# Small products of constants at the borders of stages, in a norm and between an attention's first scores, on one Trainium2 core

## What is computed

```python
def first_block(x, c, ctx, ...):
    h  = modulate(rms_norm(x, g_attn), sh_a, sc_a)
    rq, rk, rv, rg, qn, qp, kn, kp, mv = head_group_inputs(h, w_in, ...)
    y_ret = retention_mix(rq, rk, rv, rg, ...)
    y_mla = blocked_attention(q_m, concat([k_mc, k_m]), concat([mvc, mv]))
    x_mid = x + gt_a * (concat([y_ret, y_mla]) @ w_out)
    x = x_mid + gt_f * sq_relu_mlp(modulate(rms_norm(x_mid, g_ffn), sh_f, sc_f), w_ff1, w_ff2)
    return rms_norm(x, g_final)

def second_block(x, meta_tokens, ...):          # two layers
    h = rms_norm(h_res, norm_gain[li])
    f_in, q, k, v, gate = split(h @ w_in[li])
    f_out = fourier_mixer(f_in, w_fourier[li])
    s = q @ k.T * scale; p = softmax(s)          # two components for each head
    o = (p[0] - lam * p[1]) @ v
    y = concat([f_out, rms_norm(o)]) * silu(gate)
    h_res = h_res + y @ w_out[li]
```

## Time and profile before

| | us |
|---|---|
| median of 3 runs | 2792.8 (2792.77 to 2797.52) |
| the profiled execution | 2796.85 |
| its span, first to last instruction | 2795.1 |
| mean granted clock of TensorE | 0.972 |

### The profile page before, as it was taken

The page is one execution under the profiler, slowest core; times in us unless marked ns, Lnnn a source line. Parts: engine busy times, 40 slices in busy tenths (PEclk is TensorE's granted clock), DMA queues, the critical chain, the costliest instruction groups (busy, mean ns, idle before and its releaser), DMA issues. The chain is left out here.

```text
span 2795.1 us, 35915 instructions
## 1 busy us (share of the span) xinstructions
PE 2642.2 (95%) x14429; PEld 2265.9 (81%) x14429; DVE 1434.5 (51%) x2019; ACT 1054.1 (38%) x1846; POOL 456.4 (16%) x283
## 2 busy tenths in 40 slices
PE   5999869899889999999999999989999999989999
PEld 1877766899777888888888999779989999768987
DVE  5743682333457666666658423347743522326751
ACT  3412443444245334333344222157722222227740
POOL 0002201332000000000000000048820000008940
PEclk8999979999989999999999999999999999999999
DMA  5531101000211112112111233232122113233222
GB/s 234 181 132 48 41 5 53 16 1 1 106 39 53 38 61 61 44 48 61 46 53 48 92 82 82 78 78 47 43 101 106 48 42 84 57 106 74 55 83 84
DMA packets 67570, 189.46 MB, mean 68 GB/s; under 512 B 8016, under 2 KB 26832, under 8 KB 66512
## 3 DMA queue, kind: packets, MB, share of 16 engines
q1 hardware_dynamic: 67408, 187.22, 21.9%
HBM read 146.79 MB, written 16.97 MB: 59 GB/s over the span
## 5 line engine op out<-in xcount | busy, mean ns | idle before, releaser
L2649 DVE SCALAR_TENSOR_TENSOR res<-ps,gates,res 128x1024 f32<-128x1024 f32 x120 | 148.6, 1279 | 100.0 <-PE ps L2773 100.0
L1285 PE MATMUL ps<-h_hi,pf_wh 128*128 128x346 f32 (+2 forms) x800 | 187.8, 338 | 0.3
L1285 PE MATMUL ps<-h_lo,pf_wh 128*128 128x346 f32 (+2 forms) x800 | 183.0, 333 | 0.0
L2508 ACT ACTIVATE wo_wh<-ff_raw 128x512 fp32r<-128x512 f32 x120 | 75.3, 628 | 280.3 <-DVE ff_raw L2619 114.2
L1921 DVE TENSOR_REDUCE da_negmax<-ps 128x1 f32<-128x1040 f32 x136 | 167.9, 1236 | 20.9 <-PE ps L1775 14.1
L1906 POOL TENSOR_TENSOR da_E<-da_E,da_F 128x1040 f32<-128x1040 f32 x68 | 164.6, 2421 | 5.7
L2773 PE MATMUL ps<-ff_h_hi,wo_wh 128*128 128x512 f32 x512 | 157.8, 389 | 1.4 <-DVE res L2649 1.3
L1818 PE MATMUL ps<-da_aT,v 128*128 128x128 f32 (+1 forms) x1224 | 158.1, 275 | 0.7 <-ACT qk L1878 0.7
L2773 PE MATMUL ps<-ff_h_lo,wo_wh 128*128 128x512 f32 x512 | 157.7, 389 | 0.0
L2773 PE MATMUL ps<-ff_h_hi,wo_wl 128*128 128x512 f32 x512 | 157.6, 389 | 0.0
L1292 PE MATMUL ps<-h_hi,pf_wl 128*128 128x346 f32 (+2 forms) x800 | 152.4, 338 | 0.0
(11 more groups left out here) (540 smaller groups left out, 6154.9 us busy)
## 6 DMA issues: line engine op xcount, KB each, us to landing
ff_raw<-w_ff SPq DMA_DIRECT2D x48, 512.0 KB, 3.5
ada_w<-w_ada SPq DMA_DIRECT2D x16, 1024.0 KB, 7.3
ff_raw<-w_in SPq DMA_DIRECT2D x20, 512.0 KB, 4.1
pf_raw<-w_in SPq DMA_DIRECT2D x20, 512.0 KB, 4.2
wo_raw<-w_out SPq DMA_DIRECT2D x18, 512.0 KB, 4.4
residual_spill<-res SPq DMA_DIRECT2D x16, 520.0 KB, 3.1
st_q<-st_q_rounded SPq DMA_DIRECT2D x32, 260.0 KB, 5.1
ada_w<-w_ada SPq DMA_DIRECT2D x4, 2048.0 KB, 16.8
```

The lines of the kernel that those rows point to most:

```text
L1285: pe.matmul(bank(i * 2 + s, s)[c], wh[:, s, q * P:(q + 1) * P], x(q)[:, a:a + ln], start=(q == 0 and n == 0), stop=False)
L2508: act.activation(ring(wh, i), src, ACT.Copy).then_inc(s_hi, 1)
L2649: last = dve.scalar_tensor_tensor(out=res[:, m, :], in0=k.ps[:, b:b + 2, :].rearrange("p c w -> p (c w)"), scalar=gate[:, m:m + 1], in1=re ...
```

## The change

A new function issues `n` products of `k.ones` by `k.ident` into a bank. It is called at the start of stages (`before`), at their end (`behind`, in `gemm` after a wait for the last evacuation of slot 0, in `gemm_tokens` after a wait for the first five), in the norm's sums, in the feed-forward at both ends, at the start of the latent attention, and in the differential attention behind the second component's scores of the first three groups and behind the last product. In the norm the increment of `s_ssq` stays on the same product but moves into the loop.

```diff
+def busy(pe, k, bank, n):
+    for _ in range(n):
+        pe.matmul(k.ps[:, bank, 0:P], k.ones[:], k.ident[:], start=True, stop=True)
 def gemm(..., split_token=False):
+         ..., before=0, behind=0, idle_bank=7):
+                busy(pe, k, idle_bank, before)
                 loop(pe, body)
+                if behind:
+                    pe.wait_ge(freed[0], NI)
+                    busy(pe, k, 0, behind)
                 if follow:
                     follow.sums(pe, 0)
 def gemm_tokens(..., also=None):
+         ..., before=4, behind=0):
+                busy(pe, k, 7, before)
                 for g, ts in enumerate(groups):
...
+                if behind:
+                    pe.wait_ge(out_lo if split else out_hi, 5)
+                    busy(pe, k, 4, behind)
 # diff_attention, TensorE's loop
                         if i < NG:
                             pv(i, 0)
+                        else:
+                            busy(pe, k, 1, 4)
                         continue
...
                     if g < NG:
                         scores(g, 1)
+                    if i < 0:
+                        busy(pe, k, 7, 6)
 # latent_heads
+                busy(pe, k, 7, 22)
                 for g in range(NG + LAG):
 # KeptNorm.sums
             for t in range(self.NT):
                 mm = pe.matmul(k.ps[:, 5, 2 * t:2 * t + 2], src[:, t * P:(t + 1) * P], k.ones[:, 0:2], ...)
-        mm.then_inc(self.s_ssq, 1)
+            if i == 1:
+                mm.then_inc(self.s_ssq, 1)
+            busy(pe, k, 2, (2, 4)[i])
 # feed_forward
+                busy(pe, k, 5, 13)
                 first()
...
+                pe.wait_ge(join.s_x, 6)
+                busy(pe, k, 0, 5)
```

More of the change, by code:

```diff
@@ L1062, in gemm @@
 def gemm(nc, k, name, w_rows, MT, KT, xh, xl, chunks, evac_act=None, evac_dve=None, preloaded=False, then=None, load=None, norm=None,
-         follow=None, store_tile=None, side=None, first_raw=None, ahead=None, split_first=None, split_next=None, chunks_at=None, late=None, stored=None, split_token=False):
+         follow=None, store_tile=None, side=None, first_raw=None, ahead=None, split_first=None, split_next=None, chunks_at=None, late=None, stored=None, split_token=False, before=0, behind=0, idle_bank=7):
     NI = max(MT // 2, 1)
@@ L1321, in token_tiles, with gemm_tokens @@
     return k.sb(f"{name}_wh", [P, 3, N], k.ring0 + 12 * N, F32R), k.sb(f"{name}_wl", [P, 3, N], k.ring0 + 16384, F32R)
-def gemm_tokens(nc, k, name, w_rows, KT, N, xh, xl, toks, out, preloaded=False, then=None, side=None, row_scale=None, also=None):
+def gemm_tokens(nc, k, name, w_rows, KT, N, xh, xl, toks, out, preloaded=False, then=None, side=None, row_scale=None, also=None, before=4, behind=0):
     groups = [list(range(g, min(g + 5, len(toks)))) for g in range(0, len(toks), 5)]
@@ L2288, in latent_attention @@
     at0 = h0 + 4 * 5152 + MH * LT * 4
-    gemm(nc, k, "uk", rows(d["w_uk"]), MH, 2, lambda q: kh[:, q, :], lambda q: kl[:, q, :], call, preloaded=True, norm=norm, then=("mv", lambda q: d["w_mv"][q % 2 * P:(q % 2 + 1) * P, :], MH * MV, 3), side=keys,
+    gemm(nc, k, "uk", rows(d["w_uk"]), MH, 2, lambda q: kh[:, q, :], lambda q: kl[:, q, :], call, preloaded=True, norm=norm, before=14, behind=4, then=("mv", lambda q: d["w_mv"][q % 2 * P:(q % 2 + 1) * P, :], MH * MV, 3), side=keys,
          evac_act=copy_out(lambda m, a, w: kraw[:, m, a:a + w] if isinstance(m, int) else kraw[:, bass.ds(m, 1), a:a + w], call))
@@ L2292, in latent_attention @@
                 lambda q, a: kh[:, q, a:a + P], lambda q, a: kl[:, q, a:a + P],
-                list(range(0, LT, P)), lambda t: (v[:, t, :],), preloaded=True, then=("uq", rows(d["w_uq"]), 3 * P, 2))
+                list(range(0, LT, P)), lambda t: (v[:, t, :],), preloaded=True, behind=4, then=("uq", rows(d["w_uq"]), 3 * P, 2))
     qpe = k.sb("q_pe", [P, MH, L], k.res0 - 512)
@@ L3627, in project @@
             silu(act, m - 12, s, i, banks, freed, first)
-    gemm(nc, k, f"pf{li}", rows(d["w_in2"], R0), 20, KD, XH, XL, cx, evac_act=project, evac_dve=times_root, preloaded=True, norm=norm, late=norm,
+    gemm(nc, k, f"pf{li}", rows(d["w_in2"], R0), 20, KD, XH, XL, cx, evac_act=project, evac_dve=times_root, preloaded=True, norm=norm, late=norm, before=7, behind=6,
          split_first=k.split[f"pf{li}"], chunks_at=lambda m: cg if isinstance(m, int) and m >= 12 else cx,
@@ L3637, in second_layer @@
                 lambda q, a: hh[:, q * L2 + a:q * L2 + a + P], lambda q, a: hl[:, q * L2 + a:q * L2 + a + P],
-                list(range(0, L2, P)), lambda t: (v[:, t, :],), preloaded=True, side=stacks, row_scale=norm.rc, also=last_silu)
+                list(range(0, L2, P)), lambda t: (v[:, t, :],), preloaded=True, side=stacks, row_scale=norm.rc, also=last_silu, before=2, behind=8)
     yb = qk
@@ L3660, in second_layer @@
         own = [k.sb(f"pf1_first_{part}", [P, KD * P], p0 + 4096 * x, F32R)[:] for x, part in enumerate(("hi", "lo"))]
-        more = dict(follow=follow, then=("pf1", rows(d["w_in2"], 20 * P), KD * P, 2), split_next={1: own}, stored=follow.s_kept,
+        more = dict(follow=follow, behind=5, then=("pf1", rows(d["w_in2"], 20 * P), KD * P, 2), split_next={1: own}, stored=follow.s_kept,
                     store_tile=lambda m: (spill[:, m:m + 1, :], k.res[:, m:m + 1, :]) if isinstance(m, int)
@@ L3712, in project @@
         last.then_inc(freed, 1)
-    gemm(nc, k, "ina", rows(d["w_ina"]), 8, KD, XH, XL, cx, norm=n1, preloaded=True, split_first=tuple(per_slot(t) for t in k.split["ina"]), then=("inb", rows(d["w_inb"]), KD * P, 2),
+    gemm(nc, k, "ina", rows(d["w_ina"]), 8, KD, XH, XL, cx, norm=n1, before=12, behind=4, preloaded=True, split_first=tuple(per_slot(t) for t in k.split["ina"]), then=("inb", rows(d["w_inb"]), KD * P, 2),
          evac_act=project,
@@ L3717, in first_block @@
                   a0, a0 + 8 * L, k.rot1, 6)
-    gemm(nc, k, "inb", rows(d["w_inb"]), 6, KD, XH, XL, call, preloaded=True, side=BesideKeys(AdaRest(k, d, ada, k.res0, "ada2", 10, {0: [0, 1], 1: [2], 2: [3], 3: [4], 4: [5]}), turns),
+    gemm(nc, k, "inb", rows(d["w_inb"]), 6, KD, XH, XL, call, preloaded=True, before=4, behind=4, idle_bank=6, side=BesideKeys(AdaRest(k, d, ada, k.res0, "ada2", 10, {0: [0, 1], 1: [2], 2: [3], 3: [4], 4: [5]}), turns),
          then=("rv", rows(d["w_rv"]), RH * RDV, 3),
@@ L3743, in first_block @@
                                 gain=lambda q: k.a1[:, 2, q:q + 1], shift=lambda q: k.mod[:, 24 + q, 0:1])], y0, F0 + 72 * L)
-    mix_out(nc, k, d["xT"], "wo1", rows(d["w_out"]), yh, yl, cx, k.gates[:, 0, :], L, norm=split, first_raw=k.raw["wo1"], preloaded=True, follow=n2, then=("ff", rows(d["w_ff"]), KD * P, 2), split_next={})
+    mix_out(nc, k, d["xT"], "wo1", rows(d["w_out"]), yh, yl, cx, k.gates[:, 0, :], L, norm=split, first_raw=k.raw["wo1"], preloaded=True, follow=n2, before=12, then=("ff", rows(d["w_ff"]), KD * P, 2), split_next={})
     n2.keep_tiles(k.sb("ffn_in_kept", [P, 4, 4, L // 2], F0 + 40 * L), fh, fl)
```

2 lines of the change are left out of this document (1 added, 1 removed).

## The result

| | before | after |
|---|---|---|
| median, us | 2793.6 (2792.77 to 2797.52, 4 runs) | 2779.2 (2775.56 to 2783.25, 4 runs) |
| ratio to before | 1 | 0.9946, 95% interval 0.9929 to 0.9963 |
| the profiled execution | 2796.85 | 2783.25 |
| its span | 2795.1 | 2781.5 |
| mean granted clock | 0.972 | 0.986 |

The change makes the kernel 14.4 us faster. The forecast was 2774, its range 2763 to 2787. The two profiled executions lie 13.6 us apart.

The account below looks back on a forecast made before the run. TensorE, busy 95% of the span, bounds the kernel, with 112.6 us of its work at 1.2 GHz. Gains of 25.5 less costs of 6.2 give 19.3 us, so 2774 from the median; range 2763 to 2787, own range 2769 to 2779.

Parts of the forecast that it names:

- the rival of a clock that falls at a border spared before: As everything moves in time, the clock falls at such a border, 3 to 6 us: 2777 to 2780; within a 0.15 rival.
- The latent attention's train: 22 products at that stage's start take 5.7 us, first scores 0.3 us late; low-clock work 5.98 us, gain 3.0.
- The costs of trains that overshoot: Products ending after the last evacuation delay the barrier: 1.2 us behind each `pv`, 0.8 behind each attention, 0.3 behind `mv`.
- The zero at `inb`: 3.41 us at low clock gain nothing: the rotation waits for a DVE chain begun with the landing of `ada_w`.
- The time that the prediction worked out by that figure, 2786: Skill's 1% as at most 28 us against the 56.3 ceiling: 12.7 gained, 6.5 net, 2786.
- in each the products run back to back once they have begun, so the pace is TensorE's: At nine simple borders, TensorE's 30.6 us of low-clock work gains half, 15.3 us.
- the rival of gains turned into waits: DVE, not TensorE, sets the pace of the first tiles; about half of 25.5 us is lost: 2786; chance 0.09.
- The first attention: Six products behind each of the first three pairs of scores; low-clock work 8.45 us, at most 4.2, taken as 2.5.
- the caveat that ACT's exponentials release the scores: At both differential attentions' starts, faster products don't bring exponentials forward; gains cut from 4.2 and 3.0 to 2.5 and 2.0.
- The projection behind the first attention: 12.24 us at low clock; four products after the attention's 16-column ones save nothing: zero, with 6.1 as the other end.
- The announced growth of the idle ahead of the first scores: In each differential attention, idle counted from the last real product of `pv` grows from 1.6 to about 2.8 us.
- The norm: Ahead of the feed-forward, 10.80 us of low-clock work; all held 5.4, nothing held about -0.8, middle taken: 2.7.

Follow-up runs that it names:

- refill: Changed kernel plus products behind the first pair of tiles: eight in `ina`, six in `wo1`, six in the first layer's `wo2`; 2778.3 us, ratio 0.9949.

## Why the prediction came out as it did

It forecast 2774.0, the median is 2779.2: right in sign and mechanism, within the range, 5 us too hopeful, just outside its own narrow range of 2769 to 2779. By the number alone the rival of a clock that falls at a border spared before, 2777 to 2780, describes it better, and it did happen.

**What held.** The product's price: 22 products took 5.15 us, 13 took 3.14 and 8 took 2.02, 0.23 to 0.25 each at the high clock (forecast 0.26), 14 partly low 6.19, 0.44. The latent attention's train, which ends ahead of what the first scores wait for: they start 5.46 us behind ACT's first copy, as before, so the 0.3 us that it was to cost came to nothing, and they run at 2.4 GHz. (The part gave 2.4 us all the same and not 2.7.) Seven borders (`rv`, `mv`, `wo1`, both `pf`, both `pv` counted with their costs) within 0.5 us of half the low-clock work of the earlier trace rows. The costs of trains that overshoot, 1.3 and 1.4 against 1.2 behind `pv`, 0.8 and 0.6 against 0.8 behind the attentions; only behind `mv` was it double, 0.6 for 0.3. The zero at `inb`: the rotation waited longer and ended where it did. The total at the low level, 80.8 us where 60 to 90 was announced; but retention has only 20.5 of it, not most, and the stretches are gone at seven of the nine simple borders. The Trainium skill, "TensorE: Matmul & The Clock Gate", Part 1, says that warming up costs under 1% of a typical kernel's span. This kernel's traces don't agree: half of TensorE's work at the low clock is 56.3 us before, 2.0% of the span, and 34.2 us after, 1.2%. The time that the prediction worked out by that figure, 2786, is 7 us above the median, its own 2774 is 5 below.

**The step that failed: "in each the products run back to back once they have begun, so the pace is TensorE's".** This looked at the first pair of tiles alone. The pace of a stage's first two pairs is that of the slowest chain up to the second pair's first product, and in `ina` and `uk` that is ACT's rounding of the second pair's weights, for which ACT isn't free earlier since it makes the norm's tiles. The kernel before told this: the second pair of `ina` waited 0.75 us for `ina_wh` behind a first pair that had begun at half speed. Whoever had asked what the *next* product waits for would have put `ina` and `uk` at zero: 3.5 us less. That was the rival of gains turned into waits, true at two borders of nine, though it named DVE and the runs show ACT.

A wait for ACT alone doesn't say so, however. The second pair of `wo1` waited 2.32 us for ACT before and waits 2.32 us after, and the stage still gained 1.6. Before, ACT in `wo1`:

```profile
731.65 1.06 ACT L689 ACTIVATE n_sq<-res 128x1024 f32<-128x1024 f32 x1 [19.06 <-DVE res L2322]
732.62 1.04 ACT L1173 ACTIVATE wo_wh<-wo_ring 128x1024 fp32r<-128x1024 f32 x1
```

Here ACT stood idle for 19.06 us until DVE had the first pair's results (17.45 in the changed kernel), so its rounding moves with TensorE; in `ina` it had work of its own right up to it.

**A longer wait can cost more than the gain.** The prediction took the worst case of a hidden gain to be zero. In `ina` it is below: idle 2.75 and 3.1 us in place of 0.75, and the clock fell in three of four such profiles (0.0 in the fourth), 1.6 to 2.8 us lost; with idles of 1.6 and 1.7 us in two further profiles of the same code it didn't fall. The rival "the clock falls at a border which was spared before" was priced at 3 to 6 us, and it came twice, here and in `wo2`'s second pair (1.6, in five of the seven profiles that have the 128-column trains at the borders and no refill). The two together are 4.4 us in the first profile.

**Sizes off.** The first attention: 2.5 forecast, 2.8 measured at its start; the rest of its 4.2 is the DVE instruction. The second: 2.0 forecast, 0.7 measured at its start, 0.9 in all. So 6.03 us of work at the low clock gave back 0.7: the caveat that ACT's exponentials release the scores weighed more than it was priced there. The projection behind the first attention was put at zero gain because the four products end behind 16-column ones; it began at the high clock in five of eight profiles with them (-4.7 us), but not in the two of the changed kernel. The announced growth of the idle ahead of the first scores came: 1.6 to 2.9 us. The norm: 2.7 forecast, 3.9 measured, of which the kernel without these products shows 2.4 to be theirs; the announced sign, second sums of 1.8 us, came (1.95), but for another reason, as that kernel has it as well. The idle times before the low stretches were read too roughly: "nearly always" 3 to 7 us, yet the clock also fell behind 2.32 us (second pair of `wo1`), 1.71 (behind the first attention), 1.68 (its third pair of scores) and 0.91 (the second sums).

**The balance** of the first profile: `ina` 5.3 us worse than forecast, the second pair of `wo2` 1.6, the second attention 1.1, `uk` 1.0; better were the first attention by 1.7, the projection behind it by 1.3, the norm by 1.2, `rv` by 0.5. The rest is under 0.5 each; 5.6 us in all. So there is luck in how near the forecast came: of the 4.7 us on the better side, 1.4 are the DVE instruction and 1.2 the norm, where the clock now falls behind the sums, and neither is shown to be the trains' work.

## What to carry to other kernels

Where TensorE idles for some microseconds at a border and the trace shows what follows at half clock, a train of small products that ends just before the last evacuation, or just before the first operand is ready, gives back up to half of that work: about half at seven borders here, 0.7 us for 6.0 of work where exponentials release the products. What ends beyond costs its full length, 0.25 us a product. Before pricing it, look one step further: what does the second group of products wait for? If it is another engine that is busy with work of its own until then (ACT in `ina`), the gain is zero, and the longer idle may be followed by another low stretch. If that engine itself waits for TensorE's first group (ACT in `wo1`), the gain stays. Follow a gain to the end of the next stage, since it may come back as a loss there (the refill of `wo1`). And check that a step which the profile shows vanishes in a kernel without its cause: the sums of the norm did not, nor did the DVE instruction's 1.4 us hang on the trains.

## What the runs showed of the hardware

- The trains with products of two columns did not hold the clock, though at the high clock they fill nearly the same time (0.95 us for four products, 1.05 with 128 columns): 137.8 us of work at the low clock against 68.3 with 128 columns, and 112.6 with no such products at all. At the low clock they cost 0.44 each, 5.68 us for 13, where the 128-column ones held the clock and took 3.14.
- Where in a border the clock falls isn't fixed by the program: the same code showed low stretches of 3.4 and 6.8 us in the second pair of `ina` in two executions of the changed kernel, none in another kernel with the same trains ahead of it, and 0 or 10.2 us behind the first attention in kernels whose code is the same there. Per part this is up to 4 us, so parts have to be read from several profiles and the verdict from medians.
- One DVE instruction of 128x512 elements in the first attention took 2.9 us in eight profiles and 0.9 in six, at the same place in the program and with the clock high; it moves the rest of the kernel by 1.4 us.
